# Seven slots later: the second token block's layer norm, output projection and score products in a single-core hybrid decoder step

## The reference, cut to what matters

```python
x1 = layer_norm(ALPHA * x + concat(ssd(x), mlstm(x)) @ w_out)       # "mix" is the product with w_out
x2 = layer_norm(ALPHA * x1 + peer(x1))

# peer, for each token and each of 8 heads:
q = x1 @ wq;  s1 = q1 @ keys1.T;  s2 = q2 @ keys2.T                 # "scores", 2 x 128 of them
top 16 of s1, top 16 of s2, top 16 of their sums -> 16 experts, softmax gates
hid = gelu(x1 . u[expert]);   out += gate * hid * v[expert]         # rows of u and v, 16384 x 1024 each
```

## Time and profile before

| | |
|---|---|
| median of 3 runs | 3348.11 us (3344.52 to 3356.62) |
| the profiled execution's own time | 3344.52 us |
| its span | 3342.7 us |
| granted TensorE clock, mean over the span | 0.969 of full speed |
| PE busy | 3095.9 us, 93% |
| DVE busy | 2542.7 us, 76% |
| POOL busy | 1711.1 us, 51% |
| ACT busy | 936.9 us, 28% |

### The profile page before, as it was taken

How to read it: one execution, slowest core, us unless ns; L and a number is a source line. 1 busy time by engine, 2 the same in 40 slices (tenths; PEclk the granted TensorE clock), 3 DMA queues, 4 the chain that set the end, 5 groups by cost and what they waited for, 6 DMA issues and landing times.

```text
span 3342.7 us, 42480 instructions
## 1 busy us (share of the span) xinstructions
PE 3095.9 (93%) x13799; PEld 2052.6 (61%) x13799; DVE 2542.7 (76%) x5370; ACT 936.9 (28%) x2145; POOL 1711.1 (51%) x1418
## 2 busy tenths in 40 slices
PE   9999999999999889988887659999999999999998
PEld 9998887787433233333344437777677766777775
DVE  7771053888599898989889967778777777877777
ACT  3112212565111121112378761111111111111112
POOL 3243131443147677766745546555555555555553
PEclk9999999999999999999898879999999999999999
DMA  4435466678679999999989999999999999999997
GB/s 154 106 75 194 160 209 214 232 269 285 236 249 384 376 380 354 382 367 374 358 308 357 338 357 396 393 381 394 397 405 392 378 390 380 391 403 388 391 395 267
DMA packets 388784, 1074.52 MB, mean 321 GB/s; under 512 B 58824, under 2 KB 148744, under 8 KB 382176
## 3 DMA queue, kind: packets, MB, share of 16 engines
q0 software_dynamic: 186624, 679.56, 53.6%
q1 hardware_dynamic: 151280, 311.91, 26.3%
q10 hardware_dynamic: 50672, 80.51, 6.6%
HBM read 978.59 MB, written 93.11 MB: 321 GB/s over the span
## 4 chain that ended last, share of the span: by engine, by line
PE 46%; DMA 10%; DVE 8%; issue 6%; POOL 3%; ACT 1%; POOLq 0%; DVEq 0%; SPq 0%; ACTq 0%; PEldq 0%
PE PB L2361 18%; PE PB L2348 14%; DMA vbf<-in_peer_v,gixv 5%; PE PB L2324 4%; PE PB L2388 3%; PE PB L2337 3%; DMA x1d<-in_peer_u 3%; DVE ub L2009 2%; PE PB L2306 2%; POOL vbf L1737 2%; DMA ub<-in_peer_u,gix 1%; POOL ub L1737 1%; DVE ohb L1956 1%; PE PB L2432 1%; DVE oha L1954 1%
## 5 line engine op out<-in xcount | busy, mean ns | idle before, releaser
L1737 POOL DMA_INDIRECT ub<-in_peer_u,gix x640 | 695.6, 1087 | 699.4 <-DVE hid L2009 506.1
L2361 PE MATMUL PB<-vbd,wd 128*128 128x512 f32 x1536 | 680.2, 592 | 0.0
L2348 PE MATMUL PB<-xds,uts 128*128 128x384 f32 x3072 | 568.6, 339 | 0.0
L2348 PEld LDWEIGHTS PB<-xds,uts 128*128 128x128 f32 x3072 | 530.9, 189 | 0.5 <-issue 0.5
L1737 POOL DMA_INDIRECT vbf<-in_peer_v,gix x340 | 395.7, 1164 | 160.0 <-issue 99.4
L2361 PEld LDWEIGHTS PB<-vbd,wd 128*128 128x128 f32 x1536 | 282.0, 190 | 306.6 <-issue 306.6
L2388 PE MATMUL PB<-vbf,dg 128*64 128x512 f32 x1200 | 323.7, 663 | 98.9 <-DMA vbf<-in_peer_v,gixv 92.6
L1737 POOL DMA_INDIRECT vbf<-in_peer_v,gixv x300 | 326.8, 1089 | 145.5 <-issue 82.7
L1970 DVE TENSOR_TENSOR uts<-PB,uts 128x512 fp32r<-128x512 f32 x256 | 176.1, 688 | 293.7 <-ACT uts L2183 293.4
L2009 DVE CUSTOM_DVE_ANT_0 ub<-ub,x1g 128x1024 f32<-128x1024 f32 x257 | 313.6, 1224 | 37.8 <-DMA ub<-in_peer_u,gix 28.7
L2183 ACT CAST uts<-PB 128x512 fp32r<-128x512 f32 x256 | 150.0, 586 | 637.5 <-PE PB L2337 625.6
(11 more groups left out here) (427 smaller groups left out, 5103.3 us busy)
## 6 DMA issues: line engine op xcount, KB each, us to landing
vbd<-in_peer_v SPq DMA_DIRECT2D x128, 512.0 KB, 7.0
x1d<-in_peer_u SPq DMA_DIRECT2D x96, 512.0 KB, 9.3
gd_d<-stag ACTq DMA_DIRECT2D x12, 2048.0 KB, 9.9
gbd<-gd_d SPq DMA_DIRECT2D x16, 1536.0 KB, 17.9
ubd<-in_peer_u SPq DMA_DIRECT2D x32, 512.0 KB, 10.2
wtr<-in_w_tok SPq DMA_DIRECT2D x6, 2048.0 KB
tok_d<-stg ACTq DMA_DIRECT2D x48, 256.0 KB, 2.0
rb_e<-rows_d SPq DMA_DIRECT2D x8, 1536.0 KB, 11.5
```

What stands on the lines that cost most here:

```text
L1737: pool.indirect_dma_start(out=buf, out_offset=None, in_=a[table], in_offset=bass.IndirectOffsetOnAxis(ap=index, axis=0)).then_inc(done, 16)
L2348: last = T.matmul(PB[:, 6, 0:TD], uts[:, b % 2, ul, k, :], xds[:, xl, k, :], start=(k, n) == (0, 0), stop=(k, n) == (KD - 1, 2))
L2361: last = T.matmul(PB[:, 2 * d + n, :], wd[:, b % 2, d * CH:(d + 1) * CH], vbd[b % 8][:, n * 512:(n + 1) * 512], start=b == 0, stop=b == NB ...
```

## The change

Only the slots of q = 0 are touched. The six norm steps of block p = 1 move from slots 1, 2, 3, 5, 6, 8 to slots 8, 9, 10, 12, 13, 15. The products `mix(2, j)` move from slots 2 to 15 to slots 9 to 22, the transposes of p = 1 from slot 9 to 16, its score products from slots 11 to 15 to slots 18 to 22. ScalarE's root moves from slot 4 to 11, the store of x1 from 9 to 16, and the copy of the transposed x1 from 10 to 17. The work itself is the same.

```diff
-                    norm_at = (1, 2, 3, 6, 7, 11) if q else (1, 2, 3, 5, 6, 8)
+                    norm_at = (1, 2, 3, 6, 7, 11) if q else (8, 9, 10, 12, 13, 15)
                     if q + 1 < NP and at in norm_at:
                         norm1(q + 1, norm_at.index(at))
 ...
-                        if at == 4:
+                        if at == (4 if q else 11):
                             root1(q + 1)
-                        if at == (12 if q else 9):
+                        if at == (12 if q else 16):
                             act.wait_ge(s["x1"], q + 2)
                             act.dma_start(x1_d[tok(ORDER[q + 1]), :], x1[:, :]).then_inc(s["x1st"], 16)
-                        if at == (14 if q else 10):
+                        if at == (14 if q else 17):
                             evac_x1(q + 1)
 ...
                     if q == 0:
                         for j in range(16):
-                            if 2 + j * 13 // 15 == t:
+                            if 9 + j * 13 // 15 == t:
                                 mix(2, j)
-                        if t == 9:
+                        if t == 16:
                             transposes(1)
-                        if 11 <= t < 16:
-                            for i in range(32 * (t - 11) // 5, 32 * (t - 10) // 5):
+                        if 18 <= t < 23:
+                            for i in range(32 * (t - 18) // 5, 32 * (t - 17) // 5):
                                 score(1, i)
```

## The result

The changed kernel took 3365.05 us in the median of its runs (3355.55 to 3376.76), the kernel before, timed beside it, 3344.95 us (3337.13 to 3356.62). The ratio is 1.0063, 95% interval [1.0048, 1.0079]: 21 us slower. Forecast were 14 us, 3362 us, within 3349 to 3375.

A forecast was written before the change was run, and what follows sets the result against it. No single bound: TensorE to 976 us and after 1996, VectorE and DMA engines to 1700, VectorE to 1996. Lateness of 16 us at slot 28 less 2 given back makes 14: 3362 us against the median 3348.1, range 3349 to 3375.

The forecast's parts named there:

- Step 0 and the first spell: Slot 8: mix(2, 0) on TensorE must wait for the norm's first step, L1800 at 926.96; idle 9.1 us.
- The clock: TensorE after each long idle spell: it runs at its lower clock for a while and loses 2 us.
- Transposes and the second spell: Slot 16: TensorE's transposes wait for x1, finished in slot 15 at about 956.1; idle 8.7 us.
- Second v pair, GpSimd, slot 28: Pair ends at 1000.7, 22.0 us late; GpSimd's v row 6 goes at 1001.5; dot product 28 is 16 us late.
- DVE at slot 25: L1800 of block p = 2 waits for the last mix(2) at 992.7; VectorE stalls 8.7 us, included in slot 28's lateness.
- SyncE's gate transfer and ScalarE's copies at nothing: Gates for v rows 0 to 15 arrive near 970, before needed; last scores copied in slot 24; neither costs anything.
- What is given back up to slot 320: From slot 28 to 320: between nothing and all 16 us of lateness could be recovered; 2 us taken back.
- The sign that was named for it: Start of the dense part, after slot 320: near 2010 instead of 1996, lasting as long as before.
- The reason given for it: From 976 to 1700 us, DMA engines at 0.98 and VectorE at 90% leave no room to catch up.
- Rival B: After slot 23 all of TensorE's 22.0 us lateness stays or grows: 3370, up to 3374 us; chance 0.24.
- A: Loops after slot 28 have waits enough to absorb most lateness; some 4 us left, 3352 us; chance 0.18.
- C: Slots 2 to 8 come up to 4.3 us sooner, second v pair by about 982: 3344 to 3348 us; chance 0.08.

The follow-up runs named there:

- step 0 early: The changed kernel with step 0 of the norm alone back in slot 1, steps 1 to 5 in slots 9 to 15: ratio 1.0043 to the kernel before.
- the split of the scores: The changed kernel with its last 13 scores moved to slots 24 to 27, behind the second v pair: ratio 1.0051 to the kernel before.
- The split of the change: The kernel before with only TensorE's list changed, ratio 1.0029, and with only the rest of the change, ratio 1.0074.
- 16.5 in the second: The changed kernel timed again without an edit against the kernel before: ratio 1.0049.
- smaller gathers: The kernel before and the changed one, v rows of the first 300 picks at 512 values instead of 1024: 3356.36 and 3371.48 us.

## Why the prediction was right, and where it was off

*Step 0 and the first spell.* L1800 forecast for 927, found at 925.50; 29.5 us after slot 0 where the sum had 29.6. Idle 9.1 forecast, 9.25 found. Right to 0.2 us.

*The clock.* 2 us for each spell; found 2.2 behind the first (19.55 to 17.33 in the same view). Right, and on the chain only once: the first loss was hidden in the second spell.

*Transposes and the second spell.* 8.7 forecast, 8.74 found. That it is this spell which decides and the first which doesn't came out only with step 0 early.

*Second v pair, GpSimd, slot 28.* Pair's end 1000.7 forecast, about 999.5 found (997.62 and half of 3.65), which is 1000.8 in the time of the first trace, since slot 0 is 1.4 us earlier here. GpSimd's v row 6 at 1001.5 forecast, 1000.38 found; its wait just ahead is 11.99 us where some 15 were named, since it had waited 9.44 us for the first pair already. Slot 28 late by 16 forecast, 15.4 and 16.0 found. This is shown: the split of the scores moved the pair and slot 28 with it.

*DVE at slot 25.* 8.7 us stall forecast, 9.06 found, and taken in by slot 28, not added, as forecast.

*SyncE's gate transfer and ScalarE's copies at nothing.* Right in the changed kernel, since x1 is later than both. The split of the change shows that this was cover and not absence of a price: with x1 early, TensorE's list and ScalarE's copy in its new slot make slot 28 late by 9.5 us, where the list alone makes it 7.2. The prediction spoke of the cover for SyncE but not for this copy.

*"What is given back up to slot 320".* This is the step that was off: 16 us at slot 28 less 2 given back. The first half stands. Of the second the times say: 21 us in the first comparison and 16.5 in the second, so 5 and 0.5 us on top of 16, not 2 below, and 12 to 15 in all with smaller gathers. For the changed kernel nothing is seen to be given back, and a few microseconds may be added. How many is not settled: the two intervals overlap from 16 to 22 us in all, and no trace of the changed kernel without "remote" waits was had. What adds them isn't shown either; the split scores, on a chip without such waits, added 6 between slots 28 and 60. The sign that was named for it did not come: the dense part was to begin near 2010 instead of 1996, and in the first trace of the changed kernel dot product 320 stood at 2025.36 where it had been at 1994.86. That trace holds the "remote" waits, so it can't settle the size. From dot product 320 to the end of the span it took 1354.1 us, and 1347.8 and 1359.5 in the two traces of the kernel before: no difference, as forecast.

*The reason given for it*, that DMA engines at 0.98 and VectorE at 90% leave no room: the first is not needed for most of it, as the smaller gathers show. The second is not shown, and TensorE's list alone made up several microseconds with both at these values. The outcome, little or nothing given back, was right; the reason is not established.

*The size.* 14 forecast, 21 and 16.5 measured. That 3362 lies only 3 us from 3365.05 is partly luck: the base was taken as 3348.11, the median of three runs, and over eight runs it is 3344.95, so a base 3.2 us too high made up for part of a change forecast too small. Rival B's 22 us of TensorE's own lateness, at a chance of 0.24, came nearer to the first; its mechanism, that the v pairs alone set the pace, was not what the traces showed at slot 28, where VectorE was 15.4 and not 22 us late.

*The chances.* Within 0.5% had 0.59, slower by more 0.37. The ratios 1.0063 and 1.0049 lie on either side of that bound. The bound itself was too wide: it was called the least that a measurement of this kernel can tell, while the interval of the first is some 5 us to each side and both intervals lie wholly above 1.

*Rivals.* A is wrong in size: it had 4 us left, and 21 and 16.5 were measured. C is wrong at its own point: the second pair ended at 999.5, not at 982.

*What no part of it had.* TensorE's list, with the first v pair ahead of 13 scores, costs 7 us at slot 28 by itself. It did not show because the late x1 covers it.

## What to carry to other kernels

Follow a late step through its chain to the engine that fetches: here norm, product, v pair, gather, and the u row queued behind it. Of several waits in a row on one engine it is the end of the last that counts, and filling an earlier one wins nothing as long as that end stays. Two halves of a change can cost 7 and 20 us and 15 together, so a half that seems free may only be covered. And in a schedule whose engines are all near full don't count on a late start being made up: here one of 15 us stayed for 290 slots even with room on the DMA engines, while one of 7 us mostly went in one trace. Busy shares of 0.9 and more do not say which it will be.

## What the runs showed of the hardware

Chips differed more than the change: the kernel before took 3347.6 us in the median on one and 3377.4 and 3376.6 on two others, at a granted clock of 0.97 everywhere. All eight traces of the slower two hold 18 to 42 "remote" waits from 976 to 2000 us, all four of the faster one none. The first trace of the changed kernel has 24 too, although the kernel before took 3344.95 us beside it, so a slower chip is not a condition for them. What these waits are the traces don't say.

TensorE's fall to its lower clock repeated to a few tenths: after idle spells of 9.2 to 9.9 us the 40 products took 19.55, 19.41, 19.27, 19.45, 19.53 and 19.28 us in six traces, against 17.33 without a spell.
